# Mid-stage copies, second-tile splits and decay rows in a two-layer fp32 kernel on one core

## The chip, the core and the metric

The kernel runs on one core of one Trainium2 chip. The metric is the device time of one execution in microseconds (us). Before the change three timed executions took 3072.25 to 3075.27 us, with a median of 3073.08 us. A lower time is better.

## The reference

Two layers are applied to a token array x of 512 x 1024, all in float32.

```
layer 1:  xn = rmsnorm(h);  proj = xn @ w_in                     # 1024 -> 6672 columns
          y_a = pool_mixer(xa) @ w_pool_up                       # trailing means over 2, 4, 8, 16 tokens
          y_b = gated_delta_rule(conv + silu of q,k,v) @ w_dn_up # 8 heads of 128
          h = h + (sigmoid(gate_a)*y_a + sigmoid(gate_b)*y_b) @ w_mix_out
          h = h + peer_ffn(rmsnorm(h))     # 8 heads, top 16 of 16384 experts by product keys
          h = rmsnorm(h)
layer 2:  h = rmsnorm_2(x);  proj = h @ w_in_2
          x,B,C = silu(conv(xbc));  a_cs = cumsum(dt * a)        # per head, per chunk
          decay = exp(a_cs[i] - a_cs[j]) for j <= i
          y = (C B^T * decay) (x dt) + C state exp(a_cs) + d_skip x     # 16 heads of 64
          y_ssd = group_rmsnorm(y * silu(z)) @ w_ssd_proj
          y_sb  = (stick_breaking(q,k,v) * silu(z_sb)) @ w_sb_proj      # 16 heads of 64
          out = (g_ssd*y_ssd + g_sb*y_sb) @ w_out;  return x + rmsnorm_2(out)
```

## The kernel before

All weights come through one stream of tiles of 128 x 1024 floats (`raw`, four slots, loaded by SyncE). Each tile is split in two float32r tiles: ScalarE copies the high part (`split_high`, L196, tile name `split`), and VectorE, or GpSimd in two stages, subtracts it from the raw tile for the low part (`split_low`, L205). Two slots hold split tiles, so tile t can be split only when TensorE is through with tile t-2. `mm_columns` (L220 to L222) then runs 24 matmuls of 128 x 512 on a tile: high by high, high by low, low by high, for eight chunks of the 1024 inputs.

The program is a row of stages, each a block with one instruction list per engine. A stage ends with a barrier of all engines (`Program.run`; in the trace a TensorE wait for it is put down to "PEq L126"). The order of the work on an engine is the order in which the code writes it; there is no planner. The stages that the change touches, in order:

- `opening` normalises x in four blocks of 128 tokens, turns them (L325, L360, L373) and splits tiles 0 and 1 of the stream for the next stage.
- `delta_front` runs 24 convolved tiles, then 12 other tiles and the delta rule, then 4 gate tiles. In the first loop ScalarE evicts tile j to `pre` (L949), VectorE runs four convolution steps on it (L1166, L1170). Beside that runs a small chain for the decay rows: `v` (L1123), softplus on ScalarE (L926 to L934), running sums into `rows` (L1135), a turn on TensorE, two copies `sum_c` and `beta_c` (L1140, L1141), and a matmul with `last_row` (L801) that waits for these.
- `merge` (twice) makes gated sums; its first tile has 12 matmuls in the first layer, 24 in the second.
- `mix_out_norm` multiplies by w_mix_out, adds to h (L1523), normalises again (`root_vector` L276 to L234, `scale` L312, `columns` L360, `lows` L373).
- `peer_route` runs the query tiles; here GpSimd makes the low parts.
- `project_ssd`, `ssd`, `project_attention`, `stick_breaking` are the second layer. `ssd` works on eight pairs of heads. For a pair n TensorE spreads two decay rows over 128 partitions (`spread`, L3038), turns `x` (L3046), runs the first quarter of a projection tile, the output of pair n-1 (L3067, L3071), the rest of the tile, and the states (L3052). ScalarE copies `x` (L3121), takes exponentials, splits, evicts (L3135). GpSimd masks `dec` (L3142) and makes the low part of tile n+2. VectorE makes the rows to be spread, each one row of `rows` selected by a mask (`sel`, L3151), the differences `dec` (L3162), the scaled inputs (L3173, L3178), the running states (L3186, L3191), the product `attn` of `dec` and `scores` (L3197), and `y` (L3203, L3209).
- `project_attention` runs 24 tiles; on the first eight it sums squares per group, and at j == 8 one reciprocal (L3456) covers both groups, whose root (L3409) scales y.

As written before, every stage ends by splitting both tiles 0 and 1 of the next one, and the second of these splits waits for the stage's own last tile.

## Time and profile before

| what | value |
|---|---|
| median of three executions | 3073.08 us |
| the profiled execution | 3070.09 us |
| its span, first to last instruction | 3068.1 us |
| granted TensorE clock, mean | 0.986 |
| TensorE busy | 2947.8 us (96%) |
| VectorE busy | 2111.3 us (69%) |
| ScalarE busy | 1284.4 us (42%) |
| GpSimd busy | 461.6 us (15%) |

A busy share is a mean over the whole span. What TensorE waits for is read from the list of waits, each wait with what ended it. A matmul of 128 x 512 shows 0.39 us from issue to end, but in a row of them one starts every 0.23 us at the full clock, so a tile of 24 takes about 5.5 us; at a granted clock of 0.5 one starts every 0.43 us.

### The profile page before, as it was taken

The page shows a single profiled execution, that of the slowest core. Times are in us where ns is not written, and L with a number is a line of the kernel's source. Part 1 is how long each engine was busy: PE and PEld are TensorE (multiplying, and loading weights), DVE is VectorE, ACT ScalarE, POOL GpSimd, SP SyncE. Part 2 cuts the span into 40 slices and gives each one's busy share as a digit, 9 for nine tenths or more (in the row PEclk, how much of TensorE's full clock was granted, in tenths as well). Part 3 has the DMA queues.
Part 4 walks back from the last instruction along what each step waited for, and adds up shares of the span by engine and source line. Part 5 has one row for each costly group of instructions (what it writes and reads, how often), then busy time and mean ns, then how long its engine had stood idle before and what let it go on. Part 6 is the DMA issues. An engine that isn't in the chain of part 4 may idle for free. (4 is left out here: it accounts for less than half of the span.)

```text
span 3068.1 us, 42072 instructions
## 1 busy us (share of the span) xinstructions
PE 2947.8 (96%) x14292; PEld 2391.2 (78%) x14292; DVE 2111.3 (69%) x3993; ACT 1284.4 (42%) x1949; POOL 461.6 (15%) x514
## 2 busy tenths in 40 slices
PE   7999999998999899999999999999998999999998
PEld 5678876887878787788888888888886867766887
DVE  5574434445888968888898889888994584546334
ACT  4443343332367852344444444444444343444222
POOL 1013442002456720000000000000001031024000
PEclk8999999999999999999999999999999999999999
DMA  3220001332234464344333433444342211200322
GB/s 108 75 66 25 29 25 62 116 124 83 83 131 179 159 220 146 115 137 137 129 118 123 136 120 127 137 137 137 114 138 70 96 49 62 83 28 1 124 97 88
DMA packets 138193, 316.99 MB, mean 103 GB/s; under 512 B 9296, under 2 KB 74960, under 8 KB 135888
## 3 DMA queue, kind: packets, MB, share of 16 engines
q1 hardware_dynamic: 133376, 280.33, 27.6%
q10 hardware_dynamic: 4688, 34.98, 2.9%
q8 instruction: 77, 1.26, 0.2%
q14 instruction: 52, 0.43, 0.0%
HBM read 275.43 MB, written 39.85 MB: 103 GB/s over the span
## 5 line engine op out<-in xcount | busy, mean ns | idle before, releaser
L205 DVE TENSOR_TENSOR split<-raw,split 128x1024 fp32r<-128x1024 f32 x190 | 231.8, 1226 | 426.3 <-ACT split L196 425.9
L196 ACT ACTIVATE split<-raw 128x1024 fp32r<-128x1024 f32 x216 | 227.1, 1057 | 596.9 <-PE proj L222 163.4
L2289 PE MATMUL up<-up_high,weight_high 128*128 128x512 f32 x700 | 272.5, 389 | 0.0
L2291 PE MATMUL up<-up_high,weight_low 128*128 128x512 f32 x700 | 272.4, 389 | 0.0
L2290 PE MATMUL up<-up_low,weight_high 128*128 128x512 f32 x700 | 272.4, 389 | 0.0
L1963 POOL TENSOR_SCALAR hot<-count,first,gate 128x128 f32<-128x128 f32 x128 | 161.1, 1266 | 90.7 <-PE score L1817 34.7
L373 POOL TENSOR_TENSOR xl<-col,xh 128x512 fp32r<-128x512 f32 x8 | 10.0, 1268 | 1073.4 <-ACT xh L345 1073.4
L2418 PE MATMUL dt<-xh,split 128*128 128x512 f32 x416 | 162.2, 390 | 2.1 <-ACTq L2536 1.8
L2420 PE MATMUL dt<-xh,split 128*128 128x512 f32 x416 | 161.9, 389 | 0.0
L2419 PE MATMUL dt<-xl,split 128*128 128x512 f32 x416 | 161.9, 389 | 0.0
L2418 PE MATMUL down<-xh,split 128*128 128x512 f32 x416 | 161.9, 389 | 0.0
L2419 PE MATMUL down<-xl,split 128*128 128x512 f32 x416 | 161.9, 389 | 0.0
L2420 PE MATMUL down<-xh,split 128*128 128x512 f32 x416 | 161.9, 389 | 0.0
L1817 PEld LDWEIGHTS score<-hot,hot 128*128 128x128 f32 x1024 | 128.5, 193 | 37.4 <-DVE hot L2005 21.4
L1817 PE MATMUL score<-hot,hot 128*128 128x128 f32 x1024 | 137.1, 281 | 18.7 <-DVE hot L2005 11.7
L2289 PEld LDWEIGHTS up<-up_high,weight_high 128*128 128x128 f32 x700 | 131.4, 188 | 27.3
L2290 PEld LDWEIGHTS up<-up_low,weight_high 128*128 128x128 f32 x700 | 131.4, 188 | 27.3
L2291 PEld LDWEIGHTS up<-up_high,weight_low 128*128 128x128 f32 x700 | 131.4, 188 | 27.2
L220 PE MATMUL proj<-xh,split 128*128 128x512 f32 x352 | 142.5, 405 | 7.5 <-PEq L126 4.7
L2517 ACT ACTIVATE up_high<-up_sums 128x1024 fp32r<-128x1024 f32 x51 | 54.2, 1063 | 212.3 <-DVE up_sums L2357 212.3
L220 PE MATMUL query<-xh,split 128*128 128x512 f32 x320 | 135.8, 424 | 7.5 <-PEq L126 7.3
L221 PE MATMUL proj<-xl,split 128*128 128x512 f32 x352 | 138.5, 393 | 0.0
(547 smaller groups left out, 7723.1 us busy)
## 6 DMA issues: line engine op xcount, KB each, us to landing
raw<-in_stream SPq DMA_DIRECT2D x440, 512.0 KB, 3.6
gates<-stage ACTq DMA_DIRECT2D x16, 2048.0 KB, 6.7
gate<-gates SPq DMA_DIRECT2D x31, 1024.0 KB, 8.3
h<-in_x SPq DMA_DIRECT2D x4, 512.0 KB, 6.0
h<-in_x SPq DMA_DIRECT2D x1, 2048.0 KB, 8.8
h_saved<-h SPq DMA_DIRECT2D x1, 2048.0 KB, 7.5
h<-h_saved SPq DMA_DIRECT2D x1, 2048.0 KB, 7.9
rows<-h SPq DMA_DIRECT2D x4, 512.0 KB, 2.6
```

The costliest lines, as they stand in the source:

```text
L196: act.activation(g.high[t % slots], g.raw[:, t % RAW, :], ACT.Copy).then_inc(g.high_split, 1)
L205: dve.tensor_tensor(g.low[t % slots], g.raw[:, t % RAW, :], g.high[t % slots], ALU.subtract).then_inc(g.low_split, 1)
L220: pe.matmul(out, hi[:, w], xh[:, c, :], start=(c == 0), stop=False)
L221: pe.matmul(out, hi[:, w], xl[:, c, :], start=False, stop=False)
L1817: ins = pe.matmul(sb[n % 4][:, k * P:k * P + P], hot2[:, n % 4, k, :], hot1[:, n % 4, k, :], start=True, stop=True)
L1963: pool.tensor_scalar(hot1[:, n % 4, BY_VECTOR, :], count[:, :], first[:, at:at + 1], gate[:, at:at + 1], ALU.is_equal, ALU.mult).then_inc( ...
L2289: pe.matmul(bank, wh, uh, start=start, stop=False, skip_group_check=True)
L2290: pe.matmul(bank, wh, ul, start=False, stop=False, skip_group_check=True)
L2291: return pe.matmul(bank, wl, uh, start=False, stop=stop, skip_group_check=True)
L2418: pe.matmul(bank, hi[:, k], g.xh[:, c, :], start=(c == 0), stop=False)
L2419: pe.matmul(bank, hi[:, k], g.xl[:, c, :], start=False, stop=False)
L2420: last = pe.matmul(bank, lo[:, k], g.xh[:, c, :], start=False, stop=(c == DC - 1))
```

## The change

- Second tiles: a stage splits only tile 0 of the next stage. Tile 1 is split at the head of the next stage, in `merge`, `peer_route`, `ssd` and `project_attention` (in `peer_route` and `ssd` its low part on GpSimd). In `opening` both tiles stay, but stand before the last `columns`. In `mix_out_norm` tile 0's low part goes to GpSimd, and `columns` stands before `root_vector`, `lows` after `scale`.
- `delta_front` and `project_ssd`: the two copies of the turned rows stand ahead of `split_low` at step 4. In `delta_front`'s step 0 the small chain stands ahead of the split of tile 2.
- `project_ssd` makes `sums_h` and `sums_l`, the high and low part of the decay rows, once, at partitions 0 to 15 and 32 to 47. `spread` multiplies these by a one-column mask, so that `sel` and its semaphore go. Two float32 matmuls of a pair become four float32r ones.
- `ssd`: before `split_low(n + 2)` GpSimd waits for `attended` of pair n, that is for both `attn` products.
- `project_attention`: root of each group by itself, at j == 4 and j == 8.

```diff
@@ opening
-                    if t >= 2:
-                        split_high(g, act, 0, t - 2)
+                for j in range(2):
+                    split_high(g, act, 0, j)
                 norm.split_columns(act, TT - 1)
...
-                norm.columns(dve, TT - 1, weight)
                 for j in range(2):
                     split_low(g, dve, 0, j)
+                norm.columns(dve, TT - 1, weight)
@@ delta_front
-                    split_high(g, act, 0, N_CONV + f + 2)
+                    if f < N_FILL + 2 * READY - 1:
+                        split_high(g, act, 0, N_CONV + f + 2)
...
-                    split_high(g, act, 0, j + 2)
-                    if j == 0:
+                    if j:
+                        split_high(g, act, 0, j + 2)
+                    else:
                         act.activation(neg_a[0:8, :], g.heads[0:8, 0:1], ACT.Exp).then_inc(rate_made, 1)
...
                         act.activation(rows[32:40, :], rows_ps[32:40, :], ACT.Sigmoid).then_inc(soft, 1)
+                        split_high(g, act, 0, 2)
                         act.wait_ge(cleared, 1)
...
-                split_low(g, dve, 0, N_CONV + N_FILL + 5)
@@ merge
             def _(act):
+                split_high(g, act, 0, 1)
                 for p, (n, kind) in enumerate(tiles):
...
             def _(dve):
+                split_low(g, dve, 0, 1)
                 for p, (n, kind) in enumerate(tiles):
@@ mix_out_norm
                 for t in range(TT):
+                    if t == TT - 1:
+                        split_high(g, act, 0, N_OUT)
                     act.wait_ge(added, 2 * t + 2)
...
-                for c in range(2):
-                    split_high(g, act, 0, N_OUT + c)
                 norm.split_columns(act, TT - 1)
+
+            @block.gpsimd
+            def _(pool):
+                split_low(g, pool, 0, N_OUT)
...
-                        norm.columns(dve, t - 1, weight)
+                        norm.lows(dve, t - 1)
                 norm.columns(dve, TT - 1, weight)
-                for c in range(2):
-                    split_low(g, dve, 0, N_OUT + c)
@@ peer_route
             def _(act):
+                split_high(g, act, 0, 1)
...
             def _(pool):
+                split_low(g, pool, 0, 1)
@@ project_ssd
-                    split_high(g, act, 0, p + 2)
+                    if p < N_PROJ2A - 1:
+                        split_high(g, act, 0, p + 2)
...
+                    if p == 5:
+                        act.wait_ge(soft, 12)
+                        act.activation(g.sums_h[0:nh, :], g.rows[0:nh, :], ACT.Copy).then_inc(sums_high, 1)
...
+                    if p == 5:
+                        dve.wait_ge(sums_high, 1)
+                        for at in (0, 32):
+                            dve.tensor_tensor(g.sums_l[at:at + nh, :], g.rows[0:nh, :], g.sums_h[0:nh, :], ALU.subtract)
+                        dve.tensor_copy(g.sums_h[32:32 + nh, :], g.sums_h[0:nh, :])
@@ ssd
                 def spread(n):
-                    pe.wait_ge(m["selected"], 2 * n + 2)
-
                     pe.wait_ge(m["diffed"], 2 * n)
+
                     for s in range(2):
-                        pe.matmul(wide[s][:, :], g.ones[0:SSD_HEADS, :], sel[s][:, :], start=True,
-                                  stop=True).then_inc(m["spread"], 1)
+                        w = slice(32 * s, 32 * s + SSD_HEADS)
+                        one = g.mask_r[w, 2 * n + s:2 * n + s + 1].to_broadcast([SSD_HEADS, P])
+                        pe.matmul(wide[s][:, :], one, g.sums_h[w, :], start=True, stop=False)
+                    for s in range(2):
+                        w = slice(32 * s, 32 * s + SSD_HEADS)
+                        one = g.mask_r[w, 2 * n + s:2 * n + s + 1].to_broadcast([SSD_HEADS, P])
+                        pe.matmul(wide[s][:, :], one, g.sums_l[w, :], start=False, stop=True).then_inc(m["spread"], 1)
...
                     act.activation(flat(x), act_buf[:, n + SX, :], ACT.Copy).then_inc(m["x_copied"], 1)
+                    if n == 0:
+                        split_high(g, act, 0, 1)
...
-                    split_high(g, act, 0, n + 2)
+                    if n < n_pairs - 1:
+                        split_high(g, act, 0, n + 2)
+                    tile_done(g, act, 0, n)
...
             def _(pool):
+                split_low(g, pool, 0, 1)
                 for n in range(n_pairs):
...
-                    split_low(g, pool, 0, n + 2)
+                    if n < n_pairs - 1:
+                        pool.wait_ge(m["attended"], 2 * n + 2)
+                        split_low(g, pool, 0, n + 2)
...
-                        dve.wait_ge(m["spread"], 2 * n + 2)
-                        select(n + 1)
@@ project_attention
-                    if j == DC:
-                        for q in range(SSD_GROUPS):
-                            dve.wait_ge(summed, per * (q + 1))
...
-                        dve.reciprocal(t[:, :, :], v[:, :, :]).then_inc(root, 1)
+                    if j in (per, 2 * per):
+                        q = j // per - 1
+                        dve.wait_ge(summed, j)
...
+                        dve.reciprocal(t[:, q, :], v[:, q, :]).then_inc(root, 1)
```

Three places follow as the instructions stand on VectorE; the numbers in the names are those of buffers. VectorE at the start of `delta_front`, before: `split` is a low part of a weight tile (first of tile 2, last of tile 6), `v` and `rows` the small chain, `conv` the convolution, `sum_c` and `beta_c` the copies.

```order
L205 TENSOR_TENSOR split_65<-raw_64,split_65 128x1024
L1122 MEMSET rows_442 128x512
L1123 TENSOR_SCALAR v_443<-rows_22,heads_50 8x512
L1166 TENSOR_SCALAR conv_441<-pre_440,cols_49 128x512
...
L205 TENSOR_TENSOR split_65<-raw_64,split_65 128x1024
L1140 COPY sum_c_451<-front_184 128x32
L1141 COPY beta_c_452<-front_184 128x32
```

The same places on VectorE now.

```order
L1124 TENSOR_SCALAR v_443<-rows_22,heads_50 8x512
L1125 MEMSET rows_442 128x512
L205 TENSOR_TENSOR split_65<-raw_64,split_65 128x1024
L1169 TENSOR_SCALAR conv_441<-pre_440,cols_49 128x512
...
L1129 COPY sum_c_451<-front_184 128x32
L1130 COPY beta_c_452<-front_184 128x32
L205 TENSOR_TENSOR split_65<-raw_64,split_65 128x1024
```

The small chain at step 0 and the two copies at step 4 have moved ahead of the low part of their step.

VectorE at the end of `mix_out_norm`, before: from the last sum into `h` to the end of the stage; `var`, `rs`, `tmp` are the root of block 3, `rows` its scaled rows, `col` and `xl` the turned columns of block 2, then of block 3.

```order
L1523 TENSOR_TENSOR h_61<-h_61,out_211 128x512 x2
L276 TENSOR_SCALAR var_6016<-ss_6014 128x1
L278 RECIPROCAL rs_6015<-var_6016 128x1
...
L312 TENSOR_SCALAR rows_6012<-h_61,rs_6015 128x1024
L360 TENSOR_TENSOR col_6013<-turned_219,cols_49 128x512 x2
L373 TENSOR_TENSOR xl_63<-col_6013,xh_62 128x4x128 x2
L360 TENSOR_TENSOR col_6013<-turned_219,cols_49 128x512 x2
L373 TENSOR_TENSOR xl_63<-col_6013,xh_62 128x4x128 x2
L205 TENSOR_TENSOR split_65<-raw_64,split_65 128x1024 x2
```

The same stretch of VectorE now.

```order
L1531 TENSOR_TENSOR h_61<-h_61,out_211 128x512 x2
L360 TENSOR_TENSOR col_6013<-turned_219,cols_49 128x512 x2
L276 TENSOR_SCALAR var_6016<-ss_6014 128x1
L278 RECIPROCAL rs_6015<-var_6016 128x1
...
L312 TENSOR_SCALAR rows_6012<-h_61,rs_6015 128x1024
L373 TENSOR_TENSOR xl_63<-col_6013,xh_62 128x4x128 x2
L360 TENSOR_TENSOR col_6013<-turned_219,cols_49 128x512 x2
L373 TENSOR_TENSOR xl_63<-col_6013,xh_62 128x4x128 x2
```

One `col` pair stands ahead of the root, and the two low parts at the end are gone from VectorE.

VectorE on one pair of heads in `ssd`, before: from the scaled C rows (`cg`) to the next differences (`dec`).

```order
L3178 TENSOR_TENSOR cg_407_15275<-grown_401_15269,act2a_14299 128x512
...
L3151 TENSOR_SCALAR sel_399_15267<-ssd_rows_14300,head_mask_58 16x512
...
L3186 COPY st_15280<-ssd_439 128x128
L3191 SCALAR_TENSOR_TENSOR st_15280<-st_15280,ssd_last_14309,ssd_439 128x64 x4
L3197 TENSOR_TENSOR attn_405_15273<-dec_403_15271,scores_414_15282 128x512
...
L3162 TENSOR_SCALAR dec_403_15271<-wide_437,ssd_sum_14306 128x128 x4
```

The same piece now.

```order
L3205 TENSOR_TENSOR cg_408_15278<-grown_402_15272,act2a_14302 128x512
...
L3208 COPY st_15283<-ssd_439 128x128
L3213 SCALAR_TENSOR_TENSOR st_15283<-st_15283,ssd_last_14312,ssd_439 128x64 x4
L3219 TENSOR_TENSOR attn_406_15276<-dec_404_15274,scores_415_15285 128x512
...
L3189 TENSOR_SCALAR dec_404_15274<-wide_437,ssd_sum_14309 128x128 x4
```

The two selections of a pair are gone from VectorE; the rest keeps its order.

## Rows read from the trace of the kernel before

**Rows 1.** The page: busy time, share and instructions of each engine.

```profile
PE 2947.8 (96%) x14292; PEld 2391.2 (78%) x14292; DVE 2111.3 (69%) x3993; ACT 1284.4 (42%) x1949; POOL 461.6 (15%) x514
```

**Rows 2.** The page's groups: busy us, mean ns, idle before and its releaser.

```profile
L205 DVE TENSOR_TENSOR split<-raw,split 128x1024 fp32r<-128x1024 f32 x190 | 231.8, 1226 | 426.3 <-ACT split L196 425.9
L196 ACT ACTIVATE split<-raw 128x1024 fp32r<-128x1024 f32 x216 | 227.1, 1057 | 596.9 <-PE proj L222 163.4
```

**Rows 3.** TensorE's waits, whole span: total us, times, longest us.

```profile
PE query L220 <- PEq L126: 7.3, 1, 7.3
PE merge L220 <- PEq L126: 6.8, 2, 4.1
...
PE last L2875 <- DVE ssd_dt L2944: 2.8, 1, 2.8
...
PE front L801 <- DVE beta_c L1141: 2.7, 1, 2.7
PE front L220 <- DVE split L205: 2.6, 1, 2.6
PE proj L220 <- ACT act2b L3414: 2.5, 1, 2.5
```

**Rows 4.** Timeline, ScalarE then VectorE, early `delta_front`: start, length, instruction, [idle before].

```profile
50.12 0.60 ACT L949 ACTIVATE pre<-front 128x512 f32<-128x512 f32 x1
...
53.52 1.22 DVE L205 TENSOR_TENSOR split<-raw,split 128x1024 fp32r<-128x1024 f32 x1
...
70.17 1.23 DVE L205 TENSOR_TENSOR split<-raw,split 128x1024 fp32r<-128x1024 f32 x1 [2.40 <-ACT split L196]
```

**Rows 5.** Timeline, VectorE, end of `opening`.

```profile
27.90 1.29 DVE L360 TENSOR_TENSOR col<-turned,cols 128x512 f32<-128x512 f32 x2 [2.22 <-PE turned L325]
...
30.50 2.35 DVE L205 TENSOR_TENSOR split<-raw,split 128x1024 fp32r<-128x1024 f32 x2
```

**Rows 6.** Timeline, VectorE, end of `mix_out_norm`.

```profile
706.77 0.15 DVE L276 TENSOR_SCALAR var<-ss 128x1 f32<-128x1 f32 x1 [1.22 <-ACT junk L264]
...
708.84 1.28 DVE L360 TENSOR_TENSOR col<-turned,cols 128x512 f32<-128x512 f32 x2
...
714.44 2.35 DVE L205 TENSOR_TENSOR split<-raw,split 128x1024 fp32r<-128x1024 f32 x2
```

**Rows 7.** Timeline, TensorE, in `ssd`.

```profile
2473.90 1.98 PE L3038 MATMUL wide<-sel,ones 16*128 16x512 f32 x4 [0.24 <-DVE sel L3151]
...
2531.30 0.83 PE L3052 MATMUL ssd<-xleft,b_rows 128*128 128x128 f32 x6
...
2534.33 0.66 PE L3046 MATMUL ssd<-ident,x 128*128 128x128 f32 x4
...
2542.27 0.83 PE L3052 MATMUL ssd<-xleft,b_rows 128*128 128x128 f32 x6
2543.38 1.98 PE L3038 MATMUL wide<-sel,ones 16*128 16x512 f32 x4 [0.28 <-DVE sel L3151]
```

**Rows 8.** Timeline of ScalarE, VectorE and GpSimd on the same pair.

```profile
2533.00 0.62 ACT L3121 ACTIVATE x<-act2a 128x512 f32<-128x512 f32 x1
...
2533.50 2.76 DVE L3197 TENSOR_TENSOR attn<-dec,scores 128x512 f32<-128x512 f32 x2
...
2532.76 2.36 POOL L205 TENSOR_TENSOR split<-raw,split 128x1024 fp32r<-128x1024 f32 x1 [2.55 <-ACT split L196]
```

**Rows 9.** Line L3197, all of the span: shortest, median, longest ns.

```profile
L3197 DVE TENSOR_TENSOR attn<-dec,scores x16: 678/684/2879, 2475.0 to 2556.5; 128x512 f32<-128x512 f32 x16
```

**Rows 10.** Timeline, VectorE, `project_attention`.

```profile
2623.25 6.55 DVE L3456 RECIPROCAL t<-v 128x1024 f32<-128x1024 f32 x1
```

**Rows 11.** Windows: length, busy time of PE, PEld, DVE, ACT, POOL; granted clock, DMA share, GB/s.

```profile
71.60:78.20 6.60, 6.55 (x14) 3.99 (x15) 2.64 (x4) 0.00 (x0) 0.00 (x0) 0.50 0.22 79
...
1130.00:2300.00 1170.00, 1167.88 (x5138) 963.06 (x5137) 1032.53 (x1525) 481.81 (x656) 3.52 (x1) 1.00 0.40 130
...
2376.60:2380.00 3.40, 3.37 (x16) 2.81 (x17) 0.00 (x0) 0.00 (x0) 0.00 (x0) 1.00 0.45 159
```

More of the change, by code:

```diff
@@ L1119, in _ @@
                         dve.reciprocal(t[64:, :], v[64:, :]).then_inc(root, 1)
+                    if j == 0:
+                        dve.tensor_scalar(v[0:8, :], rows_ps[0:8, :], g.heads[0:8, 1:2], None, ALU.add).then_inc(soft, 1)
+                        dve.memset(rows[:, :], 0.0).then_inc(rows_cleared, 1)
+                    if j == 4:
+                        dve.wait_ge(turned, TT)
+                        cols = cols_ps[:, :].rearrange("p (c n) -> p n c", n=P)
+                        dve.tensor_copy(sum_c[:, :, :], cols[:, 0:8, :]).then_inc(tail, 1)
+                        dve.tensor_copy(beta_c[:, :, :], cols[:, 32:40, :]).then_inc(tail, 1)
                     split_low(g, dve, 0, j + 2)
-                    if j == 0:
-                        dve.memset(rows[:, :], 0.0).then_inc(rows_cleared, 1)
-                        dve.tensor_scalar(v[0:8, :], rows_ps[0:8, :], g.heads[0:8, 1:2], None, ALU.add).then_inc(soft, 1)
                     if j == 1:
@@ L2847, in project_ssd @@
     mixed = g.at("conv", R + 43, [P, 2, S])
+    g.sums_h = g.at("sums_h", R + 28, [P, S], F32R)
+    g.sums_l = g.at("sums_l", R + 29, [P, S], F32R)
     read, summed, done, cleared, silu = (g.sem(x) for x in (
         "bank_read", "conv_step", "conv_out", "pad_cleared", "silu_done"))
-    soft, turned, tail, spread, rate = (g.sem(x) for x in ("softplus", "turned", "scalars", "last_spread", "rate"))
+    soft, turned, tail, spread, rate, sums_high = (g.sem(x) for x in (
+        "softplus", "turned", "scalars", "last_spread", "rate", "sums_high"))
     with ExitStack() as stack:
@@ L2987, in flat @@
         return b[:, :, :].rearrange("p c n -> p (c n)")
-    sel = [g.at(f"sel{s}", R + 28 + s, [SSD_HEADS, S]) for s in range(2)]
     grown = [tile(f"grown{s}", 30 + s) for s in range(2)]
@@ L3179, in prepare @@
                                           ALU.mult).then_inc(m["c_scaled"], 1)
-                    if not last:
-                        dve.wait_ge(m["spread"], 2 * n + 2)
-                        select(n + 1)
                     dve.wait_ge(m["states_made"], n + 1)
```

56 lines of the change are left out of this document (26 added, 30 removed).

## The prediction

> **What bounds the kernel now.** I read the busy times first. TensorE is busy for 2947.8 of 3068.1 us [rows 1], so the kernel goes as fast as TensorE is fed, and a change pays only where it takes a wait or work from TensorE. Next I read what TensorE waits for [rows 3]. The reader is to see two kinds of row. Waits put down to "PEq L126" stand at stage boundaries: 7.3 us ahead of the query tiles, 4.1 us ahead of the first `merge`. The others stand inside a stage: 2.8 us for `ssd_dt`, 2.7 us for `beta_c`, 2.6 us for a low part, 2.5 us for an eviction. Third I read the timelines around these, for what stood ahead of the instruction that was waited for. Last comes the granted clock [rows 11]: 1.00 in the long expert stretch, but 0.50 for the 6.6 us right after the wait for `beta_c`. TensorE had idled 2.7 us before; while its clock is half, every matmul takes twice its step. The wait for `ssd_dt` was as long, yet the clock after it stays at 1.00. So a removed wait is worth its length for certain, and the slow stretch behind it only sometimes.
>
> The Trainium skill, page TensorE: Matmul & The Clock Gate, section What's actually happening, says that the activity check runs free and is not started by the kernel, so that the same wait need not always be followed by the low clock. The two waits of rows 11 agree. By that rule closing a wait guarantees no clock back, which is why I count the clock in part.
>
> **The change part by part.** All sums are against the profiled execution, 3070.09 us (span 3068.1 us, 2 us around it). The median of the timed runs lies 3.0 us above it; I add the same 3.0 us at the end.
>
> *End of `opening`.* Two low parts of together 2.35 us are the stage's last work [rows 5]. They move into the 2.22 us in which VectorE waits for TensorE ahead of the last columns. Their high parts come earlier on ScalarE too, 1.06 us each [rows 2], after the columns of block 2, and that also frees ScalarE between blocks. Gain 2.2 to 3.3 us; I take 2.4.
>
> *Step 0 of `delta_front`.* ScalarE evicts tile 0 (`pre`) only at 50.12, because its softplus chain with three table loads began after tile 0; the low part of tile 3 then stands behind tile 0's convolution, at 53.52 [rows 4], and TensorE waits 2.6 us [rows 3]. Now the chain runs beside tile 0. The next candidate is the convolution of tile 0, which ends some 7 us earlier, so the low part of tile 3 waits for tile 1 alone and is there a tile ahead. Gain 2.6 us.
>
> *Step 4 of `delta_front` and of `project_ssd`.* The two copies stood behind a low part that waits for tile 4 itself (start 70.17 [rows 4]): high, low, copies, all with TensorE idle. The rows that they copy were turned a tile earlier. Ahead of that low part the copies are done during tile 4, and tile 5 is already split. Gain 2.7 and 2.8 us. The new split of the decay rows in step 5 (one copy on ScalarE, three short instructions on VectorE, each at most the 1.23 us of a low part) falls into VectorE's wait for the next high part, 2.40 us even where a convolution runs in every step [rows 4], and `project_ssd` has none in its first eight; at worst it costs 1 us.
>
> *Second tiles.* From TensorE's last matmul to the barrier stood one high part, 1.06 us, and one low part, 1.23 us [rows 2], with 0.1 us of latency: 2.4 us. Where only these two lie at the end (`delta_front`), all of it goes. In `project_ssd` and `project_attention` an eviction stays behind the last tile, so I take 1.4 and 1.8 us. At the end of `ssd` the last output and `y` are later anyway: 0. At the heads the same 2.4 us lie beside tile 0's matmuls, 24 x 0.23 = 5.5 us (0.23: 1167.88 us over 5138 matmuls, nearly all of 512 columns [rows 11]), or 2.7 us where tile 0 has 12 (first `merge`); with GpSimd's 2.36 us for a low part [rows 8] it is 3.5 us against 5.5. If that cover is gone, a head gives its gain back. The low part of tile 2 isn't held up, since it waits for tile 0 in any case.
>
> *End of `mix_out_norm`.* Of the 7.3 us wait, VectorE's two low parts, 2.35 us, go. The `columns` of block 2, 1.28 us, move into the 1.22 us in which VectorE waits for the squares of block 3 [rows 6]. Block 2 is turned only after the last output tile, so they start about 1 us into that wait and hold up the root by 0.3 us, and the low parts of block 2 come beside block 3's turn. Gain 3.6 us; with nothing gained by the move 2.4.
>
> *`ssd`.* Three things change on a pair. (a) The spread, 1.98 us [rows 7], becomes four float32r matmuls of 0.23 us: 0.9 us or less. It no longer waits for `sel` either (0.28 us). (b) VectorE loses the two selections. (c) GpSimd's low part, 2.36 us, ran from 2532.76; the two `attn` began at 2533.50 and took 2.76 us [rows 8], where their median is 0.684 us each [rows 9]. So the first stood about 1.4 us for GpSimd. Now the low part comes after them. Queued behind it on GpSimd are the masks of the next pair, which `attn` of that pair needs; low part, two masks (under 1.6 us each by my estimate from the low part's 2.36 us for twice the columns) and two `attn` make a ring of 2.36 + 3.2 + 1.4 = 7 us, under the present period of 10.97 us (2531.30 to 2542.27 [rows 7]). VectorE then needs about 8.7 us a pair, so TensorE and ScalarE are late next. After a tile ScalarE splits, evicts and copies `x`: the copy ended at 2533.62 [rows 8], 2.3 us after the states began. The turn needs it. It stood at 2534.33 and now can start at about 2533.67; from the turn to the next states it is 7.94 us [rows 7]. New period 2.37 + 7.94 = 10.3 us. The spreads at 2473.90 and 2543.38 are six periods apart: 69.5 us, 11.6 each, as some periods hold a stretch at half clock. At 10.3 they make 61.8, a gain of 7.7 us; if the slow stretches stay, 4. The first pair gains 1.4 us (its own spread), the last about 1.5 to 2.5. In all 10 us, from 5 to 13.
>
> The Trainium skill, page SBUF — State Buffer, section Who interferes with whom, says that a VectorE instruction with two SBUF inputs and a GpSimd one that reads SBUF shut each other out for a whole instruction, while one with a single SBUF input doesn't contend. Rows 8 and 9 agree for `attn`. By this rule the low part in its new place leaves the differences (read from PSUM) alone, but the masks, now later, would stand against the gating of `y` and the scaled C rows, which read SBUF twice: the block could move and not go. That is the first rival below.
>
> *`project_attention`.* One reciprocal of 1024 columns takes 6.55 us [rows 10]; VectorE's next low part and ScalarE's root, and so an eviction, come late by 2.5 us [rows 3]. In halves, 3.3 us lies in step 4 and 3.3 us in step 8, and each fits between two low parts of a 5.5 us tile. The second half ends 3.3 us before the present one, more than the wait is long, so all of it can go unless ScalarE's table loads around the root hold up the eviction: 1.2 to 2.5 us, I take 2.4.
>
> *Sum of the waits and the work:* 2.4 + 2.6 + 2.7 + 2.8 + 2.4 + 1.4 + 1.8 + 3.6 + 10 + 2.4 = 32.1 us.
>
> *The clock.* The stretch after `beta_c` costs 6.6 x 0.5 = 3.3 us. If it goes alone, 3.3; if the shorter ones behind the other closed waits go too, up to 10; if they only fall elsewhere, 0. I take 5, so 37 us in all: 3070.1 - 37 + 3 = 3036 us.
>
> **The rivals.** *A: the waits go, the rest doesn't.* In `ssd` VectorE stands for GpSimd's masks as long as it stood for the low part, and TensorE's low-clock stretches reappear elsewhere. For: rows 9, and the free 1.00 after one wait of two. Against: the masks have 1.2 us of slack a pair. `ssd` then gives only 3 us and the clock 0: 3073 - 25 = 3048 us.
>
> *B: all of it.* `x` is copied in time, the period of a pair falls to TensorE's own 9.4 us (7.94 + 0.83 + 0.66), which gives 13 us over six and 17 in all, and every slow stretch goes, 10 us: 3073 - 49 = 3024 us. Against: the copy of `x` stands behind a split and an eviction on ScalarE.
>
> *C: no change.* The stream, not the splits, would set the pace, and every closed wait would come back as a wait for a tile. For: one stream feeds all. Against: the DMA share is 0.40 in the expert stretch at a TensorE busy for 1167.88 of 1170 us [rows 11]. 3073 us.
>
> *D: slower.* GpSimd's low part waits for `attended`, and tile n+2 with it; the ring above becomes the period. It decides from 10.3 us on; to eat the other gains and 7 us more it must reach 15 us a pair, (15 - 11.6) x 7 = 24 us worse in place of 10 better, with half of the other 27 us lost to heads whose second tile comes late: 3073 + 24 - 14 = 3083 us. The ring's 7 us speaks against it.
>
> **How the numbers follow.** Forecast 0.62, its own range 3028 to 3044; A 0.22; B 0.08; C 0.05; D 0.03. The range is 3025 to 3052: it holds the forecast, most of A and the near part of B. A measurement of this kernel can tell a change from none at about 0.2%, 6 us. Faster by more: forecast, A and B, 0.92. Within: C, 0.05. Slower: D, 0.03.
>
> **What would show it.** In the changed kernel's list of waits the rows for `ssd_dt`, `beta_c`, the low part in the front and the eviction in `project_attention` must be gone or under 0.5 us, the wait ahead of the query tiles at 3.3 to 4.5 us, the one ahead of the first `merge` near 1.8 us. The `attn` must show a longest of about 0.7 us, and the spreads must stand 10.1 to 10.6 us apart. `ssd` is wrong if a period stays near 11, with `y` or `cg` lengthened (A), or if TensorE waits for a low part there (D). The heads are wrong if TensorE waits at a stage's second tile. The prediction fails if the sum of TensorE's waits falls by the 22 us and the time does not.

## The result and the profile after

The changed kernel took 3025.46 us (median of 3021.43 to 3029.74 us, four executions), the kernel before on the same chip 3073.65 us (3072.25 to 3075.27). The ratio is 0.9841, with a 95% interval of 0.9826 to 0.9856: 48.2 us faster where 37 were forecast. The median lies half a microsecond above the lower edge of the range, 3025 us; by the ratio, 0.9841 of the 3073.08 us that the forecast started from, it is 3024.2 us, just below that edge.

The traced execution of the changed kernel took 3027.81 us (span 3025.7 us), 42.3 us under that of before. First the page's busy line; it answers [rows 1].

```profile
PE 2922.6 (97%) x14292; PEld 2379.9 (79%) x14292; DVE 2090.9 (69%) x3979; ACT 1284.5 (42%) x1950; POOL 468.0 (15%) x516
```

TensorE runs as many matmuls as before and is busy 25.2 us less. A part, 10.1 us, is the shorter spread of the decay rows (8 x (1.98 - 0.72)), the rest is the clock. Next come two rows of TensorE's list of waits before the change, which [rows 3] does not show (total us, times, longest us), and then the list of the changed kernel, which answers [rows 3].

```profile
PE attn L3512 <- PEq L126: 3.6, 1, 3.6
PE prep L220 <- PEq L126: 3.3, 1, 3.3
```

```profile
PE ssd L3072 <- ACT x L3147: 6.9, 7, 1.6
...
PE merge L220 <- PEq L126: 4.6, 2, 2.7
...
PE query L220 <- PEq L126: 2.9, 1, 2.9
...
PE prep L220 <- PEq L126: 1.8, 1, 1.8
...
PE attn L3537 <- PEq L126: 1.8, 1, 1.8
```

The rows for `ssd_dt`, `beta_c`, the low part in the front and `act2b` are gone. The wait ahead of the query tiles fell from 7.3 to 2.9 us, a little under the 3.3 to 4.5 us that the prediction had named. One large row is new: TensorE waits for ScalarE's copy of `x`, 6.9 us in `ssd`.

The next two views show windows by stage, from a stage's first matmul to that of the next: length, busy time of PE, PEld, DVE, ACT, POOL, granted clock, DMA share, GB/s. First the kernel before: `delta_front`, `ssd`, `project_attention`, `stick_breaking`.

```profile
34.21:523.66 489.45, 465.41 (x2591) 367.13 (x2591) 249.54 (x372) 197.40 (x323) 126.79 (x124) 0.97 0.13 44
2462.03:2561.63 99.60, 92.97 (x553) 67.64 (x553) 88.70 (x200) 38.58 (x62) 42.04 (x24) 0.95 0.12 43
2561.63:2719.99 158.36, 152.20 (x656) 120.89 (x657) 61.05 (x56) 61.49 (x78) 5.14 (x20) 0.99 0.24 80
2719.99:2840.35 120.36, 115.44 (x545) 75.67 (x545) 71.29 (x73) 51.18 (x41) 51.39 (x108) 0.97 0.00 1
```

The same four stages of the changed kernel:

```profile
33.08:508.62 475.54, 459.06 (x2591) 363.54 (x2591) 248.44 (x371) 196.44 (x322) 126.79 (x124) 0.99 0.14 46
2437.89:2527.95 90.06, 79.54 (x552) 62.38 (x553) 69.30 (x184) 37.66 (x61) 42.40 (x24) 0.98 0.14 47
2527.95:2680.43 152.48, 150.57 (x656) 119.74 (x657) 61.29 (x57) 61.65 (x78) 5.14 (x20) 1.00 0.25 83
2680.43:2797.87 117.44, 112.53 (x544) 74.57 (x545) 71.26 (x73) 51.17 (x41) 51.34 (x108) 1.00 0.00 1
```

Read the second number, PE's busy time. In `delta_front` 2591 matmuls are busy 465.41 us before and 459.06 after. The work is the same, so 6.35 us of the stage's 13.9 us are clock. `stick_breaking`, whose own waits stayed at 4.9 us, gives 2.9 us, all clock.

Last a pair of heads in `ssd` (start, length, instruction, [idle before]), TensorE, ScalarE, VectorE and GpSimd in turn; it answers [rows 7, 8].

```profile
2491.45 0.50 PE L3061 MATMUL wide<-sums_h,mask_r 16*128 16x512 f32 x2
2491.78 0.39 PE L3065 MATMUL wide<-sums_l,mask_r 16*128 16x512 f32 x2
2493.06 0.66 PE L3072 MATMUL ssd<-ident,x 128*128 128x128 f32 x4 [0.89 <-ACT x L3147]
...
2501.69 0.50 PE L3061 MATMUL wide<-sums_h,mask_r 16*128 16x512 f32 x2
...
2490.95 1.06 ACT L196 ACTIVATE split<-raw 128x1024 fp32r<-128x1024 f32 x1 [4.27 <-PE prep L222]
2491.91 0.58 ACT L3165 ACTIVATE act2b<-prep 128x512 f32<-128x512 f32 x1
2492.39 0.62 ACT L3147 ACTIVATE x<-act2a 128x512 f32<-128x512 f32 x1
...
2492.78 1.29 DVE L3219 TENSOR_TENSOR attn<-dec,scores 128x512 f32<-128x512 f32 x2
2494.10 2.16 DVE L3189 TENSOR_SCALAR dec<-wide,ssd_sum 128x128 f32<-128x128 f32 x8
...
2494.15 2.38 POOL L205 TENSOR_TENSOR split<-raw,split 128x1024 fp32r<-128x1024 f32 x1 [4.92 <-DVE attn L3219]
```

The two `attn` take 1.29 us together. GpSimd's low part starts right behind them, beside the differences. The spread, from 2491.45 to 2492.17, is 0.72 us where it was 1.98. The spreads stand 10.24 us apart, as forecast (10.3), and the turn waits 0.89 us for the copy of `x`, as forecast too (10.3 less the 9.4 us that rival B gives as TensorE's own period).

### The profile page after: what moved, and what is told of

Same layout as the page of the kernel before. It is cut to its first block and busy times, and to the rows that moved or that the text cites. A ratio compares the mean times of both kernels' runs of the same rounds, so it can differ in the third digit from the quotient of the medians.

```text
span 3025.7 us, 42053 instructions
## 1 busy us (share of the span) xinstructions
PE 2922.6 (97%) x14292; PEld 2379.9 (79%) x14292; DVE 2090.9 (69%) x3979; ACT 1284.5 (42%) x1950; POOL 468.0 (15%) x516
## 3 DMA queue, kind: packets, MB, share of 16 engines
q1 hardware_dynamic: 133376, 280.33, 27.9%
## 5 line engine op out<-in xcount | busy, mean ns | idle before, releaser
L205 DVE TENSOR_TENSOR split<-raw,split 128x1024 fp32r<-128x1024 f32 x188 | 229.4, 1225 | 402.0 <-ACT split L196 401.5
L2637 DVE TENSOR_TENSOR split<-raw,split 128x1024 fp32r<-128x1024 f32 x102 | 124.9, 1224 | 20.1 <-ACT split L2509 20.0
```

Source lines behind the costliest of these rows:

```text
L205: dve.tensor_tensor(g.low[t % slots], g.raw[:, t % RAW, :], g.high[t % slots], ALU.subtract).then_inc(g.low_split, 1)
L2637: dve.tensor_tensor(g.low[j % 2], raw(k), g.high[j % 2], ALU.subtract).then_inc(d_low, 1)
```

## The experiments

All kernels are edits of the changed kernel unless said otherwise. A median is compared with 3023.56 us, the changed kernel's in the first group of runs. An interval is some 4 to 6 us to either side, so the stages of the traces tell more than the medians.

**The changed kernel again, and the kernel before again.** No edit.

> The changed kernel once more, unedited, timed against the kernel before in five rounds. It serves as the base of the other runs of this chip. The theory: the forecast missed because the clock term was 5 us where 11 to 15 us came back, and because the profiled execution of before lay 3.5 us under its own median; then the ratio is 0.984 to 0.987 again, 40 to 49 us under before, and TensorE's half-clock stretches behind the closed waits stay away. The rival: the surplus over the 37 us forecast was scatter of four runs; then the difference is 35 to 39 us.

> The kernel before, unedited, for a second trace of it. The theory: the half-clock time inside delta_front (12.6 us of loss in the first trace, 3.4 to 6.8 us in the eight traces with its two waits closed) hangs on the two waits, so it is 10.5 to 14 us again, at the same two places; the stretches in the stages that the change left alone (routing, experts, last merge) move by 1 to 4 us. The rival: the first trace had caught an unlucky front, and this one shows 5 to 8 us there.

> The changed kernel for a third trace. Two traces agree on ssd (90.0 us), project_attention (152.5) and stick_breaking (117.4) with little or no half clock there. If the kernel sets the places, the same again within 0.2 us; if they are free, at least one of the three is 1.7 us or more longer.

The changed kernel took 3023.56 us, ratio 0.984 (0.9826 to 0.9853), 49.4 us under before, so the surplus is no scatter of four runs. Its three traces, the third on another chip, differ though nothing changed: `delta_front` starts at 33.08, 30.94 and 33.16 us, and `ssd` takes 90.06, 90.01 and 88.46 us, while `project_attention` and `stick_breaking` repeat to 0.02 us. The second trace of before (3073.94 us) lies 3.9 us over the first, and 3.7 of that is `ssd`, here with the row of `delta_front` ahead of it.

```profile
34.14:523.61 489.47, 465.41 (x2590) 367.08 (x2591) 249.46 (x372) 197.53 (x323) 126.86 (x124) 0.97 0.14 44
2461.90:2565.23 103.33, 97.22 (x553) 70.53 (x553) 84.78 (x200) 38.50 (x62) 41.00 (x24) 0.91 0.13 41
```

`delta_front` repeats to 0.02 us, clock and all. `ssd` has the same work at a mean clock of 0.91 where it was 0.95: TensorE is busy 4.25 us longer.

**The two reorders of `delta_front`, undone.** `front_undo` takes back both, `front0_undo` the small chain at step 0, `front4_undo` the copies at step 4.

```diff
@@ front0_undo: ScalarE, then VectorE
-                    if j:
-                        split_high(g, act, 0, j + 2)
-                    else:
+                    split_high(g, act, 0, j + 2)
+                    if j == 0:
...
-                        split_high(g, act, 0, 2)
@@ front4_undo: VectorE (moved behind split_low(j + 2))
                     if j == 4:
                         dve.wait_ge(turned, TT)
...
                         dve.tensor_copy(beta_c[:, :, :], cols[:, 32:40, :]).then_inc(tail, 1)
```

> The changed kernel, but in delta_front the small chain of step 0 and the two copies of step 4 stand behind their splits again. Both theories: TensorE's two waits of 2.6 and 2.7 us come back, 5.3 us. The clock theory adds the half-clock stretches that stood behind them before (the front's matmuls were busy 465.4 us before and 459.1 us after, though their number is the same): 5 to 7 us, so 10 to 12 us over the changed kernel. The rival, that waits alone made the gain of the front and the clock's stretches only fall elsewhere: 5 us over the changed kernel.

> The changed kernel, but in delta_front the small chain of step 0 alone stands behind the split of tile 2 again. Both theories: the wait for tile 3's low part comes back, 2.6 us. The clock theory: a stretch at half clock stands at that wait again (3.4 us long, 1.7 us of loss, in both traces that had the wait), so delta_front takes 479 to 481 us against 475.5, 4 to 5 us over the changed kernel in the median. The rival: 2.6 us.

> The changed kernel, but in delta_front the two copies of step 4 alone stand behind the low part again. Both theories: the wait for beta_c comes back, 2.7 us. The clock theory: a stretch at half clock stands right behind it (6.8 us long in the trace of before, 3.4 us in that with both waits back), so delta_front takes 480 to 482 us against 475.5, 5 to 7 us over the changed kernel in the median. The rival: 2.7 us.

> The changed kernel with only the two copies of step 4 put back, for a second trace. The first had the wait of 2.7 us, a stretch of 3.4 us at half clock behind it, and yet less half clock in delta_front as a whole (3.4 us of loss against 5.1), so the stage cost 1.5 us more and not 2.7. If the places are set by the kernel, 477.0 us again; if they are free, anything from 477 to 482 us.

The medians were 3036.57 us (ratio 0.9858 to 0.9893), 3035.65 us (0.9856 to 0.9896) and 3026.35 us (0.9833 to 0.986). With both undone TensorE's list of waits has these two rows again,

```profile
PE front L801 <- DVE beta_c L1142: 2.7, 1, 2.7
PE front L220 <- DVE split L205: 2.6, 1, 2.6
```

and the window of `delta_front` reads

```profile
31.61:519.66 488.05, 466.26 (x2591) 368.07 (x2591) 248.43 (x371) 196.57 (x322) 126.93 (x124) 0.97 0.14 44
```

The stage is 12.5 us longer than in the changed kernel: 5.3 us of waits, and 7.2 us of busy time (466.26 against 459.06) that only the clock can explain. With step 0 alone:

```profile
31.20:514.36 483.16, 464.12 (x2591) 365.53 (x2591) 248.25 (x371) 196.58 (x322) 126.88 (x124) 0.98 0.14 45
```

That is 7.6 us, 2.6 of them wait and 5.1 clock. With step 4 alone, the stage and the stretch right behind its wait:

```profile
31.02:508.01 476.99, 457.80 (x2591) 362.72 (x2591) 248.45 (x371) 196.32 (x322) 126.81 (x124) 0.99 0.14 45
...
63.80:67.21 3.41, 3.41 (x8) 2.22 (x8) 1.65 (x3) 0.00 (x0) 0.00 (x0) 0.50 0.38 142
```

The wait is back with its slow stretch, yet the stage is only 1.5 us longer, because other slow stretches later in it are gone (457.80 us busy against 459.06). The second trace says the same, 476.95 us. So my expectations for step 0 (479 to 481) and step 4 (480 to 482) were both wrong: the wait's own length comes back each time, the clock does not come back wait by wait. The two parts alone make 9.1 us, together 12.5, but the stage's clock also moves without any edit in it: in the twelve traces that have both reorders it is busy from 455.94 us (second trace of `no_attended`) to 460.65 us (`spread_undo`). Against these the clock of step 0 (464.12) and of both (466.26) stands out, that of step 4 alone (457.80) does not. And not all of step 0's lies at its wait: of its slow stretches one of 3.41 us stands there, at 50.49 us, and one of 13.65 us stands at 494.23 us, where the changed kernel has 6.83 us.

**Second tiles split at the tails again.** `heads_undo`, in all stages that the change touched.

```diff
@@ merge, peer_route, ssd, project_attention (heads; low parts alike)
-                split_high(g, act, 0, 1)
@@ project_attention (tails of the others alike)
-                    if j < N_PROJ2B - 1:
-                        split_high(g, act, 0, j + 2)
+                    split_high(g, act, 0, j + 2)
```

> The changed kernel, but every stage splits both tiles 0 and 1 of the next stage at its own end again (in mix_out_norm the second low part on GpSimd, behind the first). By the waits alone: 2.3 us ahead of the first merge, 1.9 us ahead of stick_breaking, 1.4 us ahead of ssd, up to 2.4 us ahead of the query tiles, 8 us in all. The clock theory adds stick_breaking's stretch of 6.8 us at half clock (2.9 us of busy time) and half of the stretches at the first merge and the query tiles, 1.7 us each: 13 to 15 us over the changed kernel. The rival: 6 to 8 us.

3032.66 us (ratio 0.9853 to 0.9883), 9.1 us over the changed kernel, between the two expectations. The waits come back as forecast:

```profile
PE merge L220 <- PEq L126: 6.8, 2, 4.1
...
PE query L220 <- PEq L126: 3.7, 1, 3.7
PE attn L3525 <- PEq L126: 3.6, 1, 3.6
PE prep L220 <- PEq L126: 3.3, 1, 3.3
```

Only the query tiles return less (0.8 us, 2.4 expected). `stick_breaking` takes 119.79 us, 2.3 more than the changed kernel's, with the same waits inside. Whether the wait at its head owns that clock is the question of the next two runs.

**GpSimd without its wait.** `no_attended`, traced twice.

```diff
                     if n < n_pairs - 1:
-                        pool.wait_ge(m["attended"], 2 * n + 2)
                         split_low(g, pool, 0, n + 2)
```

> The changed kernel, but GpSimd's low part in ssd no longer waits for the attention product. If that low part (2.4 us) shuts the products out, the first of each pair's two attn takes about 2.1 us in place of 0.68 again, the output stands 0.4 to 0.5 us later on TensorE, ScalarE's eviction and copy of x follow, and the period goes from 10.25 to 10.7 us: 3 to 4 us over the changed kernel. The rival: ScalarE's copy of x sets the period whatever VectorE does, and the wait was worth nothing: 0 to 1 us, with lengthened attn all the same.

> The changed kernel without GpSimd's wait in ssd, for a second trace. Its first trace lost 6.8 us to half clock at the head of stick_breaking, a stage that it does not touch and whose waits are the same 4.9 us as in the changed kernel, where the loss is 0. If the place of the slow stretches is set by the kernel, stick_breaking takes 123 to 124 us again; if it is free from one execution to the next, 117.4 to 121 us.

3038.01 us (ratio 0.9877 to 0.991). The timeline of VectorE and TensorE on one pair:

```profile
2488.76 2.90 DVE L3218 TENSOR_TENSOR attn<-dec,scores 128x512 f32<-128x512 f32 x2
...
2491.76 0.66 PE L3093 MATMUL ssd<-attn,xdt 128*64 128x128 f32 x8 [0.67 <-issue]
```

The products take 2.90 us in place of 1.29, the output stands 0.67 us for them (the profile names no releaser, but the second product ends at 2491.66, 0.10 us ahead of it), and `ssd` takes 95.0 us (94.8 in the second trace) against 90.0. The spreads are 10.98 us apart, the period of before (I had expected 10.7). The Trainium skill, page SBUF — State Buffer, section Who interferes with whom, has a VectorE instruction with two SBUF inputs contend with a GpSimd one that reads SBUF; the 2298 ns of the first product agree, and so do the differences, read from PSUM, which in the changed kernel keep their 2.16 us beside the low part.

That explains 5 us. `stick_breaking`, which this edit does not touch, explains part of the rest; its window in the first and in the second trace of this kernel:

```profile
2679.08:2802.65 123.57, 118.66 (x544) 77.86 (x545) 71.25 (x73) 51.16 (x41) 50.77 (x108) 0.94 0.00 1
```

```profile
2681.44:2798.87 117.43, 112.52 (x544) 74.58 (x545) 71.27 (x73) 51.17 (x41) 51.34 (x108) 1.00 0.00 1
```

One kernel, one stage, the same waits: 6.1 us apart by the clock alone. The second execution, on another chip, took 3028.82 us, and lost 1.6 us in `project_attention`, where the first had lost nothing (152.18 us busy against 150.56). The other timed executions (3037 to 3040 us) have no trace, so their remainder stays open. The Trainium skill, page TensorE: Matmul & The Clock Gate, section What's actually happening, says that the activity check runs by itself and is not started by the kernel; that one kernel shows both rows fits this, and does not prove it.

**The spread undone, and both of `ssd`'s edits undone.** `spread_undo` puts back `sel` and the float32 matmuls, `ssd_undo` also takes the wait away.

```diff
-                        pe.matmul(wide[s][:, :], one, g.sums_h[w, :], start=True, stop=False)
...
+                        pe.matmul(wide[s][:, :], g.ones[0:SSD_HEADS, :], sel[s][:, :], start=True,
+                                  stop=True).then_inc(m["spread"], 1)
```

> The changed kernel, but the decay rows are spread as before: two selections on VectorE and two float32 matmuls of together 1.98 us a pair; GpSimd's wait stays. If the spread stands on the path, the turn starts 0.7 us later than the copy of x allows (2 x 0.99 us behind a wait of 0.28 us), and the period goes from 10.25 to 10.9 us, the period of before: 5 to 7 us over the changed kernel with the first pair. The rival: GpSimd's wait made the gain, and the shorter spread only let TensorE wait for x: 0 to 2 us.

> The changed kernel with both of ssd's edits undone, GpSimd's wait and the short spread. Undone alone the first lengthened ssd from 90.0 to 95.0 us, the second to 98.5 us. The theory, that the two stand side by side and either alone sets the old period: about 98 us again, 8 us over the changed kernel, no more than the larger of the two. The rival, that each has its own share of the path: 5.0 + 8.5 us, ssd at 103 to 104 us.

3035.5 us (ratio 0.9867 to 0.9904) and 3033.04 us (0.9854 to 0.9884). `ssd` takes 98.5 and 98.1 us. TensorE with the old spread and GpSimd's wait:

```profile
2483.16 1.98 PE L3053 MATMUL wide<-sel,ones 16*128 16x512 f32 x4 [0.60 <-DVE sel L3173]
2485.07 0.77 PE L3061 MATMUL ssd<-ident,x 128*128 128x128 f32 x4
...
2494.47 0.83 PE L3067 MATMUL ssd<-xleft,b_rows 128*128 128x128 f32 x6
```

From the second spread on they are 11.2 to 12.1 us apart, where I had expected 10.9. Here TensorE waits 0.60 us for `sel`, spreads for 1.98 us, and its list of waits has none for `x`. With both undone `ssd` is no slower than with the spread alone, so the shares of 5.0 and 8.5 us do not add to 13.5: beside the old spread GpSimd's wait is worth nothing, and the short spread gets its last 5 us only with the wait. Some of this is clock: TensorE's busy time in `ssd` is 1.4 and 1.9 us above the changed kernel's and the longer spread's 10.1 us.

**Three edits in three stages, undone together.** `late_undo`: `mix_out_norm`, the copies in `project_ssd`, the reciprocal.

```diff
@@ project_ssd: moved behind split_low(p + 2)
                     if p == 4:
                         dve.wait_ge(turned, TT)
@@ project_attention
-                    if j in (per, 2 * per):
+                    if j == DC:
```

> The changed kernel with three of its edits undone in three stages that the stage table keeps apart: mix_out_norm's order and its low part on VectorE, project_ssd's two copies behind the low part of step 4, project_attention's reciprocal in one piece. By the waits: 2 us ahead of the query tiles, 2.8 us in project_ssd, 2.5 us in project_attention, 7 to 8 us in all. The theory that a slow stretch of TensorE's clock stands behind some waits and not others: no half clock behind the last two, as before, so 7 to 9 us over the changed kernel. The rival, every such wait brings its own slow stretch as in delta_front (3.5 us each): 13 to 16 us.

3036.8 us (ratio 0.9868 to 0.9903), 13.2 us over the changed kernel. The waits are the ones that the prediction named:

```profile
PE query L220 <- PEq L126: 5.3, 1, 5.3
...
PE last L2882 <- DVE ssd_dt L2956: 2.8, 1, 2.8
PE proj L220 <- ACT act2b L3431: 2.5, 1, 2.5
```

That is 2.4 + 2.8 + 2.5 = 7.7 us. In `project_attention` the clock takes 1.6 us more (152.16 us busy against 150.57), where the same wait before the change had no slow stretch near it (its own, with 152.20 us, stood at the stage's head). That 1.6 us is no price of this wait: five other edited kernels that keep the split reciprocal, `spread_undo` one of them, are busy 152.2 us there too. Inconclusive between the two expectations: the waits are certain, and the rest of the 13 us is clock in touched and untouched stages.

The four groups undone, `front_undo`, `heads_undo`, `ssd_undo` and `late_undo`, lie 13.0, 9.1, 9.5 and 13.2 us over the changed kernel in their medians. Together these are 44.8 of the 49.4 us; only the edit of `opening` is in none of them. With 4 to 6 us of doubt on each this is a rough check, and no large part is missing.

**`x` copied early.** `x_early`, traced twice; `both` also puts one of `opening`'s low parts behind the last columns.

```diff
@@ x_early: ScalarE in ssd
                 for n in range(n_pairs):
-
-                    act.wait_ge(m["x_turned"], n)
-                    act.activation(flat(x), act_buf[:, n + SX, :], ACT.Copy).then_inc(m["x_copied"], 1)
...
                     if n < n_pairs - 1:
+                        copy_x(n + 1)
                         split_high(g, act, 0, n + 2)
@@ both: VectorE in opening
-                for j in range(2):
-                    split_low(g, dve, 0, j)
+                split_low(g, dve, 0, 0)
                 norm.columns(dve, TT - 1, weight)
+                split_low(g, dve, 0, 1)
```

> The changed kernel, but ScalarE copies x of the next pair right after the exponentials of dec, ahead of the next high part and eviction. If ScalarE's copy ahead of the turn sets the period (TensorE waits 0.89 us for it on seven pairs, 1.55 us on the first), the spreads stand 9.4 us apart in place of 10.25, those waits are gone, and the time is 6 to 7 us under the changed kernel. The rival: VectorE is next in line (its instructions of a pair add up to 8.9 us in a chain) and the period stays at 10 us: 2 us under the changed kernel or none.

> The changed kernel with the early copy of x in ssd, and in opening only one of the two low parts ahead of the last columns, the other one behind them. By the theory the last columns start 1.2 us sooner and the front too, so 1 to 1.5 us under the kernel with the early copy of x alone, 6 to 8 us under the changed kernel. The rival: the second low part, now last, holds up the end of opening by as much: equal to the early copy alone.

> The changed kernel with the early copy of x, for a second trace. The work: ssd at 82.5 us in any case. The first trace lost 1.7 us each in project_attention and stick_breaking and 4.7 us in the last merge to half clock, where the same kernel with one more edit in opening lost 0, 0 and 1.7 us. If the kernel sets the places: the same losses again. If they are free: others.

`x_early` took 3018.12 us (ratio 0.9809 to 0.9844), in one more execution 3018.08 us. TensorE there:

```profile
2479.27 0.50 PE L3061 MATMUL wide<-sums_h,mask_r 16*128 16x512 f32 x2
2479.60 0.39 PE L3065 MATMUL wide<-sums_l,mask_r 16*128 16x512 f32 x2
2479.92 0.66 PE L3072 MATMUL ssd<-ident,x 128*128 128x128 f32 x4
...
2488.63 0.50 PE L3061 MATMUL wide<-sums_h,mask_r 16*128 16x512 f32 x2
```

The turn follows the spread at once, the period is 9.36 us, and `ssd` takes 82.5 and 82.6 us in the two traces. So ScalarE's copy did set the period. By the medians it is 5.4 us under the changed kernel; the intervals overlap, the traces of `ssd` do not. The slow stretches moved again: the first trace is busy 1.6 us longer in `project_attention` and 1.4 in `stick_breaking`, the second in neither.

`both` took 3021.40 us (ratio 0.9825 to 0.9854), no better than `x_early`. VectorE at the end of its `opening`:

```profile
24.62 1.23 DVE L205 TENSOR_TENSOR split<-raw,split 128x1024 fp32r<-128x1024 f32 x1 [0.32 <-ACT split L196]
26.57 1.29 DVE L360 TENSOR_TENSOR col<-turned,cols 128x512 f32<-128x512 f32 x2 [0.72 <-PE turned L325]
...
29.16 1.22 DVE L205 TENSOR_TENSOR split<-raw,split 128x1024 fp32r<-128x1024 f32 x1
```

The columns come sooner, at 26.57, and the second low part is now the last work: the rival was right, and the front starts at 31.74 us, inside the spread of the unedited kernel.

## Why the prediction was wrong in size

The 48.2 us are 42.3 us from trace to trace, 3.6 us by which before's trace lay under its median, and 2.35 us by which the changed kernel's lay over its own. The forecast had carried the 3.0 us between before's trace and its median over to the changed kernel. So the 10.5 us between 3036 and 3025.46 us are two misses of about the same size: 5.3 us in the sum of the terms (42.3 against 37), and 5.35 us in this carried term (3.0 + 2.35).

| term | forecast us | measured us |
|---|---|---|
| end of `opening` | 2.4 | 1.1, 3.3, 1.1 in three traces |
| step 0 and step 4 of `delta_front` | 5.3 | 5.3 |
| second tiles, three heads | 5.6 | 5.6 (2.28 + 1.44 + 1.86) |
| end of `mix_out_norm` | 3.6 | 4.1 (idle in the stage, 10.57 to 6.51) |
| step 4 of `project_ssd` | 2.8 | 2.8 |
| `ssd`, its clock included | 10 | 9.5; 13.3 against before's second trace |
| reciprocal | 2.4 | 2.5 |
| clock elsewhere | 5, at most 10 | 11.8 |

*What failed is the clock term,* and with it the 3.0 us carried over. The step read: "The stretch after `beta_c` costs 6.6 x 0.5 = 3.3 us ... if the shorter ones behind the other closed waits go too, up to 10 ... I take 5." Measured by TensorE's busy time for the same matmuls it is 6.35 us in `delta_front`, 2.9 in `stick_breaking`, 1.6 in `project_attention`, and 0.9 net in all others: 11.8 us outside `ssd`. Any of the two traces of before against any of the three of the changed kernel gives 11.0 to 12.2 us outside `ssd`, so the size is no chance of one pair. The measured terms make 42.7 us, with `opening` at 1.1. I had priced one stretch by its row, and rightly: 6.55 us busy at half the clock, 3.3 us. I guessed at the others, though before's windows show them at the waits that were to be closed. Two more stand in `delta_front`, at its head and behind the wait of step 0:

```profile
34.20:37.00 2.80, 2.79 (x7) 2.25 (x8) 0.17 (x2) 0.00 (x0) 0.00 (x0) 0.50 0.58 176
54.70:57.60 2.90, 2.81 (x7) 2.26 (x8) 2.83 (x8) 1.00 (x2) 0.00 (x0) 0.50 0.53 171
```

Half of each is 1.4 us; with the 3.3 us of [rows 11] that is 6.1 of the stage's 6.35 us. `stick_breaking` has such a stretch of 6.83 us at its head, and `project_attention` one of 3.41 us near its head, where the wait hardly changed (2.6 to 2.3 us); both are gone too. To count all half clock of before as gain would have been far too much: its mean of 0.986 over 3068.1 us lacks 43 us, and the changed kernel's 0.992 still lacks 24.

`ssd` holds 3.3 us more of the clock. Of its 13.4 us of busy time 10.1 are the spread, 8 x (1.98 - 0.72). In before's second trace it is 7.6 us. That trace lies near the median, so the 3.0 us that the forecast carried over were, as far as two traces show, slow clock in `ssd` that the first trace had missed. In the changed kernel that stage takes 88.5 to 90.1 us in all three traces; there was nothing to carry over.

*The waits* came out as named, to within half a microsecond each but for `opening`, and the undone kernels bring each back at its forecast length, but for the one ahead of the query tiles: the second tile returns 0.8 us of it, `mix_out_norm` 2.4, together 3.2 of the 4.4 us. In `opening` the two low parts ahead of the last columns hold these up until 27.56 (27.90 in [rows 5]). Between 1.1 and 3.3 us the place of a slow stretch seems to decide: it lies at 27.9 and 28.1 us in the traces that start the front at 33.08 and 33.16, at 22.5 us in the one that starts it at 30.94. No kernel with this edit alone undone was run.

*`ssd`* was right in its mechanism and its period. I had not seen that the two edits need each other, since I summed (a), (b) and (c) in one chain; the runs with one of them undone show it. Which instruction passes the one's delay on to the other was not traced.

*The rivals.* A is refuted: `y` (0.75 us) and `cg` (1.28 us for two) are as short as before, and the gating of `y` takes 0.71 us where it took 0.87. It was close: on the pair shown the masks end at 2499.48 and `cg` begins at 2499.58, and the first pair's product did stand 0.7 us for a mask, 1421 ns against 684, where the prediction had named a longest of about 0.7 us. B came near the measured time in part by luck: its clock of 10 us did come back (11.8), but its 17 us in `ssd` did not, since the period stayed at 10.24 us until `x_early` brought it to 9.36. C is refuted by the time. D is refuted, no low part is late.

*The [rows 9] and [rows 10] of the changed kernel* close the reading (shortest, median, longest ns):

```profile
L3219 DVE TENSOR_TENSOR attn<-dec,scores x16: 678/685/1421, 2447.5 to 2523.1; 128x512 f32<-128x512 f32 x16
...
L3481 DVE RECIPROCAL t<-v x2: 3352/3352/3353, 2562.1 to 2587.4; 128x512 f32<-128x512 f32 x2
```

What stays open: why a slow stretch lasts 3.4 us in one trace and 6.8 or 13.7 in another, and how much of `stick_breaking`'s 2.9 us is the closed wait at its head. All three traces with that wait at its full 3.6 us lost 2.3 to 2.9 us of busy time in the stage; of the fifteen with 1.8 us three lost 1.4, 1.4 and 6.1 us, and the others nothing.

## What to carry to other kernels

Waits that one reads off the list, with what stands ahead of the late instruction, could here be summed to half a microsecond, most of them. For the clock, list every slow stretch that stands at a wait to be closed and price them all, half of the busy time in each, on more than one trace; a wait put back alone does not bring back a fixed amount, as the same stage moved by up to 4.7 us among traces with the same code. A gap between a trace and its median can be such clock as well, and is then no constant to add. Where two edits shorten one ring of work, undo each alone before giving either a price: here one was worth nothing beside the old form of the other. And look at what is late next in the changed trace, since the 0.89 us wait that the forecast had named was the next 7.5 us of `ssd`.

## What the runs showed of the hardware

Two float32r matmuls of 16 rows on different partitions (0 to 15 and 32 to 47) ran side by side: the second two of a spread show 0.39 us together, as long as one, and all four took 0.72 us from the first start to the last end, where four in a row at 0.23 us apart would take 1.08 (3 x 0.23 + 0.39). No run put them on the same partitions, so that the partitions are the reason is not shown.

The granted clock repeats in some places and differs from one execution to the next in others. `delta_front` before the change lost the same in two traces (465.41 us busy in each), and in every trace with one of its two waits open a stretch at 0.50 stood at that wait. In the twelve traces with both closed none stands between 5 and 170 us into the stage, where both waits had been. `ssd`'s clock in the same two traces was 0.95 and 0.91, and `stick_breaking`'s in two traces of another kernel 0.94 and 1.00.

A wait of 0.89 us on each of six pairs in a row (after 1.6 us on the first) did not lower the clock in all of `ssd`: one of the changed kernel's three traces shows no half clock there at all.
